# One decoder layer on one core: MLP products by one level of Strassen, projection in two column passes, activation sums kept in HBM

## What is computed

```
h   = h + concat(y_conv, y_ret) @ w_out          # 1024 x 1024
hn2 = rmsnorm(h, norm_mlp)
h   = h + square(relu(hn2 @ w_up)) @ w_down      # 1024 x 4096, 4096 x 1024
y   = rmsnorm(h, norm_final)                     # meta tokens dropped
```

## Time and profile before

| what | value |
|---|---|
| median of 3 runs | 1241.77 us (1241.03 to 1242.4) |
| span of the profiled execution, first to last instruction | 1239.3 us |
| input stages, up to the projection | 0 to 402.8 us |
| output projection | 402.8 to 493.3 us |
| MLP with the end | 493.3 to 1239.3 us |
| busy in the span: PE, DVE, ACT, POOL | 98%, 45%, 27%, 18% |
| DMA moved, mean rate | 70.35 MB, 57 GB/s |

### The profile page before, as it was taken

The page is one execution under the profiler, slowest core; times in us unless marked ns, Lnnn a source line. Parts: engine busy times, 40 slices in busy tenths (PEclk is TensorE's granted clock), DMA queues, the critical chain, the costliest instruction groups (busy, mean ns, idle before and its releaser), DMA issues.

```text
span 1239.3 us, 19873 instructions
## 1 busy us (share of the span) xinstructions
PE 1219.2 (98%) x7759; PEld 1195.8 (96%) x7759; DVE 556.0 (45%) x943; ACT 333.5 (27%) x667; POOL 224.3 (18%) x144
## 2 busy tenths in 40 slices
PE   8999999999999999999999999999999999999997
PEld 7889998999999999999999999999999999999997
DVE  4345455464455655643343343343333343343345
ACT  5412313224125333320321321311311311311324
POOL 0144243252231223911011010010010010010000
PEclk9999999999999999999999999999999999999999
DMA  5331211311311112121111111111111111111103
GB/s 190 125 86 51 71 51 35 86 51 36 85 35 37 52 34 85 34 69 51 52 50 36 51 51 47 38 51 51 34 51 51 42 43 51 51 49 36 34 18 120
DMA packets 101225, 70.35 MB, mean 57 GB/s; under 512 B 2477, under 2 KB 97417, under 8 KB 101187
## 3 DMA queue, kind: packets, MB, share of 16 engines
q1 hardware_dynamic: 96415, 67.42, 17.8%
q10 hardware_dynamic: 4772, 2.40, 0.7%
HBM read 63.18 MB, written 6.64 MB: 56 GB/s over the span
## 4 chain that ended last, share of the span: by engine, by line
PE 95%; DVE 3%; ACT 1%; issue 1%; DMA 0%; SPq 0%; POOL 0%; DVEq 0%; POOLq 0%; ACTq 0%
PE bank L1004 29%; PE bank L1006 28%; PE bank L1005 28%; PE bank L1037 1%; PE bank L1038 1%; PE bank L1040 1%; DVE state L870 1%; PE bank L1094 1%; PE bank L1099 1%; PE bank L1096 1%; PE bank L1108 1%; PE bank L1132 1%; PE bank L1201 1%; DVE rstd_b L941 1%; PE bank L1020 1%
## 5 line engine op out<-in xcount | busy, mean ns | idle before, releaser
L1004 PE MATMUL bank<-x_hi,w_hi 128*128 128x344 f32 (+2 forms) x1344 | 435.4, 324 | 2.1 <-DVE h_f L944 1.8
L1006 PE MATMUL bank<-x_hi,w_lo 128*128 128x344 f32 (+2 forms) x1344 | 430.2, 320 | 0.0
L1005 PE MATMUL bank<-x_lo,w_hi 128*128 128x344 f32 (+2 forms) x1344 | 429.5, 320 | 0.0
L1004 PEld LDWEIGHTS bank<-x_hi,w_hi 128*128 128x128 f32 x1344 | 252.2, 188 | 4.4 <-DVE w_lo L706 1.9
L1005 PEld LDWEIGHTS bank<-x_lo,w_hi 128*128 128x128 f32 x1344 | 252.5, 188 | 0.3
L1006 PEld LDWEIGHTS bank<-x_hi,w_lo 128*128 128x128 f32 x1344 | 252.5, 188 | 0.0
L1005 PE MATMUL bank<-mid_lo,w_hi 128*128 128x344 f32 (+3 forms) x720 | 230.7, 320 | 0.0
L1006 PE MATMUL bank<-mid_hi,w_lo 128*128 128x344 f32 (+3 forms) x720 | 230.3, 320 | 0.0
L1004 PE MATMUL bank<-mid_hi,w_hi 128*128 128x344 f32 (+3 forms) x720 | 229.8, 319 | 0.0
L390 POOL TENSOR_TENSOR w_raw<-w_raw,prm 128x1024 f32<-128x1024 f32 x56 | 109.3, 1957 | 590.1 <-DMA w_raw<-w_up_dram 540.7
L481 ACT ACTIVATE w_hi<-w_raw 128x1024 fp32r<-128x1024 f32 x94 | 98.9, 1053 | 378.7 <-PE bank L1006 374.3
(11 more groups left out here) (147 smaller groups left out, 1079.1 us busy)
## 6 DMA issues: line engine op xcount, KB each, us to landing
w_raw<-w_up_dram SPq DMA_DIRECT2D x32, 512.0 KB, 3.9
w_raw<-w_down_dram SPq DMA_DIRECT2D x32, 512.0 KB, 3.4
w_raw<-w_in_dram SPq DMA_DIRECT2D x28, 512.0 KB, 3.6
w_raw<-w_out_dram SPq DMA_DIRECT2D x8, 512.0 KB, 3.5
x_raw<-x_prompt_dram SPq DMA_DIRECT2D x7, 512.0 KB, 3.5
y_prompt_dram<-y_out SPq DMA_DIRECT2D x7, 512.0 KB, 2.6
state<-state_ret_dram SPq DMA_DIRECT2D x4, 512.0 KB, 5.0
v_bc<-v_smp_dram SPq DMA_DIRECT2D x4, 512.0 KB, 6.5
```

The costliest lines, as they stand in the source:

```text
L1004: m_.matmul(out, sh, mh, start=i == 0, stop=False)
L1005: m_.matmul(out, sh, ml, start=False, stop=False)
L1006: ins = m_.matmul(out, sl, mh, start=False, stop=i == len(pairs) - 1)
```

## The change

**Projection.** The 1032 columns are now two halves of 516 (HALF), and each half two parts of 258 (TQ). The projection goes over all 8 output tiles for part t = 0 of both halves, then again for part t = 1. So it loads and splits w_out twice (16 tiles, 32 groups of 24 matmuls with 258 columns). h is kept in `hid` and saved to HBM (h_dram). While the second pass runs, GpSimd, ScalarE and VectorE normalise the t = 0 part and make the seven combined operands that Strassen's method (Winograd's form) needs of it, hi and lo of each. Those of t = 1 are made in the first up passes.

**Up.** w_up and hn2 are taken as 2 x 2 blocks: hidden features by halves, input features by halves, tokens by halves. One unit is two hidden tiles (u and u + 16). GpSimd makes four sums of the weight blocks (`up_sum`), ScalarE and VectorE hi and lo of seven operands in single slots (`up_split`, `up_low`). TensorE does seven steps of 12 matmuls for each part t, accumulating in three PSUM bank pairs (BANK), and ScalarE and VectorE combine the results into the four blocks of the hidden activations while the steps go on. There are 18 passes: units 0 and 1 in two narrow passes each (one part t), units 2 to 15 in one wide pass each (both parts). After a pass ScalarE applies Relu and Square, GpSimd makes the four sums of blocks that the down products need (`mid_sum`), and SP stores the seven operands to HBM (m_dram).

**Down.** 8 blocks (of 4 hidden tiles) x 4 pairs of output tiles, 7 steps of 6 matmuls for each part. The last block is done for t = 0 first and then for t = 1. Weights are combined in the same way (`down_sum`, `down_split`, `down_low`), and the block's seven operands are loaded back from HBM through two slots (`load_mid`) and split (`mid_split`, `mid_low`). VectorE adds every step's result into the accumulators. For block 0 it adds h, loaded back from HBM, instead.

**Norm gain and factor** are applied to the activations before the up products; the gain on the weights is gone. **End:** ten groups of tokens; three are finished between the last down passes, seven after the last.

The core of the diff, in this order: constants, SP with its loads and stores, GpSimd, ScalarE (the up passes, then the down passes), VectorE (mid_low, the up passes, the down passes), TensorE (the up passes, the down passes):

```diff
+A_OP = ((0, 0), 1, (0, 1), 2, 0, (1, 1), 3)
+BANK = (0, 1, 0, 1, 2, 1, 2)
+STARTS = (True, True, False, False, True, False, False)
+UNITS = DFF // P // 2
+UP = [(0, (0,)), (1, (0,)), (1, (1,)), (0, (1,))] + [(u, (0, 1)) for u in range(2, UNITS)]
+NU = len(UP)
+UP_S = [0, 1, 1, 2] + list(range(3, NU - 1))
+BLOCKS = 8
+DN = [(b, n, (0, 1)) for b in range(BLOCKS - 1) for n in range(4)] + [(BLOCKS - 1, n, (t,)) for t in range(2) for n in range(4)]
+ND = len(DN)
...
+            def load_up(u):
+                for i in range(2):
+                    c0 = P * (u + UNITS * i)
+                    sp.dma_start(up_raw[u % 2][:, i, :, :], w_up_t[:, :, c0:c0 + P]).then_inc(up_in[u % 2], 16)
...
+            def store_rest(q):
+                u, ts = UP[q]
+                c0, c1 = TQ * ts[0], TQ * (ts[-1] + 1)
+                sp.wait_ge(mid_sums, 4 * q + 4)
+                sp.dma_start(m_dram[u, :, 1:7, c0:c1], hid[:, 1:7, META + c0:META + c1]).then_inc(rest_saved, 16)
...
+            def load_mid(m):
+                b, j = m // 7, m % 7
+                sp.wait_ge(first_saved, 16 * (2 * b + 4))
+                sp.wait_ge(rest_saved, 16 * (2 * b + 4))
+                if m >= 2:
+                    sp.wait_ge(mid_ready, 2 * m - 2)
+                sp.dma_start(m_raw[m % 2][:, :, :], m_dram[2 * b:2 * b + 2, :, j, :].rearrange("u p c -> p u c")).then_inc(mid_in[m % 2], 16)
...
+            for q in range(NU):
+                if q:
+                    store_rest(q - 1)
+                if q == 3:
+                    sp.wait_ge(up_ready, 7 * (last_pass(0) + 1))
+                    load_up(2)
+                if q >= 4:
+                    u = q - 2
+                    if u + 1 < UNITS:
+                        sp.wait_ge(up_ready, 7 * (last_pass(u - 1) + 1))
+                        load_up(u + 1)
+                if q < NU - 1:
+                    store_first(q)
+            sp.wait_ge(up_ready, 7 * NU)
+            load_down(0)
+            load_mid(0)
+            load_mid(1)
+            load_down(1)
+            for i in range(4):
+                load_h(0, i)
+            for m in range(2, 7):
+                load_mid(m)
+            store_first(NU - 1)
+            store_rest(NU - 1)
+            for wi in range(NW):
+                b, n = wi // 4, wi % 4
+                if wi + 2 < NW:
+                    sp.wait_ge(dn_ready, 7 * wi + 7)
+                    load_down(wi + 2)
+                if b < BLOCKS - 1:
+                    for j in range(2 * n, min(2 * n + 2, 7)):
+                        load_mid(7 * (b + 1) + j)
...
+            def mid_sum(q):
+                u, ts = UP[q]
+                c0, c1 = META + TQ * ts[0], META + TQ * (ts[-1] + 1)
+                b12 = hid[:, 3, HALF + c0:HALF + c1]
+                b11, t2, b21, t3, t1, t4, b22 = (hid[:, j, c0:c1] for j in range(7))
+                pool.wait_ge(mid_set, 4 * q + 4)
+                g.tensor_tensor(t1, b12, b11, ALU.subtract).then_inc(mid_sums, 1)
+                pool.wait_ge(mid_sums, 4 * q + 1)
+                g.tensor_tensor(t2, b22, t1, ALU.subtract).then_inc(mid_sums, 1)
+                g.tensor_tensor(t3, b22, b12, ALU.subtract).then_inc(mid_sums, 1)
+                pool.wait_ge(mid_sums, 4 * q + 2)
+                g.tensor_tensor(t4, b21, t2, ALU.subtract).then_inc(mid_sums, 1)
...
+            up_sum(1)
+            block_sums(1)
+            for q in range(1, NU):
+                mid_sum(q - 1)
+                if q + 1 < NU and UP_S[q + 1] != UP_S[q]:
+                    up_sum(q + 1)
+            down_sum(0)
...
+            for q, (u, ts) in enumerate(UP):
...
+                for i in range(7):
+                    if i == 0:
+                        act.wait_ge(up_done, 7 * q + 1)
+                        if q in (0, 2):
+                            act.wait_ge(normed, 8 * (ts[0] + 1))
+                            act.wait_ge(h_saved[ts[0]], 32)
+                        if q:
+                            act.wait_ge(up_read, 5 * (q - 1) + 4)
+                        s.activation(split(hid[:, 0, HALF + c0:HALF + c1]), pair[0][:, tsl, 0:TQ], ACT.Copy).then_inc(up_x_read, 1)
+                    if i == 2:
+                        act.wait_ge(up_done, 7 * q + 3)
+                        if q:
+                            act.wait_ge(mid_sums, 4 * q)
+                            act.wait_ge(first_saved, 16 * q)
+                        s.activation(split(hid[:, 0, c0:c1]), pair[0][:, tsl, 0:TQ], ACT.Relu).then_inc(up_x_read, 1)
+                        act.wait_ge(up_x_read, 2 * q + 2)
+                        s.activation(hid[:, 0, c0:c1], hid[:, 0, c0:c1], ACT.Square).then_inc(mid_set, 1)
+                    if q + 1 < NU:
+                        up_split(q + 1, i)
+                        if q == 0 and i == 2:
+                            std_rows(1)
...
+            for q, (b, n, ts) in enumerate(DN):
+                for i in range(7):
+                    if q + 1 < NW:
+                        down_split(q + 1, i)
+                    if b < BLOCKS - 1 and i in (1, 4) and 2 * n + i // 4 < 7:
+                        mid_split(7 * (b + 1) + 2 * n + i // 4)
...
+            def mid_low(m, half):
+                b, j = m // 7, m % 7
+                dve.wait_ge(mid_high, m + 1)
+                d.tensor_tensor(m_lo[b % 2][j][:, half, :], m_raw[m % 2][:, half, :], m_hi[b % 2][j][:, half, :], ALU.subtract).then_inc(mid_ready, 1)
...
+                for i in range(7):
+                    if i == 1:
+                        dve.wait_ge(up_done, 7 * q + 2)
+                        dve.wait_ge(up_x_read, 2 * q + 1)
+                        d.tensor_tensor(u2, yb, s1, ALU.add).then_inc(up_read, 1)
+                    if i == 3:
+                        dve.wait_ge(up_done, 7 * q + 4)
...
+                    if q + 1 < NU:
+                        up_low(q + 1, i)
...
+                for i in range(7):
+                    src = pair[BANK[i]][:, tsl, 0:TQ]
+                    dve.wait_ge(dn_done, 7 * q + i + 1)
...
+                    if b < BLOCKS - 1 and i in (2, 3, 5, 6) and 2 * n + i // 5 < 7:
+                        mid_low(7 * (b + 1) + 2 * n + i // 5, (i - 2) % 3)
...
+            for q, (u, ts) in enumerate(UP):
+                for i in range(7):
+                    pe.wait_ge(up_ready, 7 * q + i + 1)
+                    if i == 0:
+                        if q:
+                            pe.wait_ge(up_x_read, 2 * q)
+                        else:
+                            pe.wait_ge(h_done, GROUPS - 1)
+                    elif i == 2:
+                        pe.wait_ge(up_x_read, 2 * q + 1)
+                    elif i in (1, 4) and q:
+                        pe.wait_ge(up_read, 5 * q - (1 if i == 1 else 0))
+                    elif i == 3:
+                        pe.wait_ge(up_read, 5 * q + 1)
+                    elif i >= 5:
+                        pe.wait_ge(up_read, 5 * q + i - 3)
+                    for t in ts:
+                        if q < 4:
+                            pe.wait_ge(op_ready, 7 * t + i + 1)
+                            if t == 1 and q == 2:
+                                pe.wait_ge(h_done, GROUPS)
+                        ins = product(pair[BANK[i]][:, t, 0:TQ], [up_hi[i][:, k, :] for k in range(4)], [up_lo[i][:, k, :] for k in range(4)],
+                                      [b_hi[t][i][:, k, :] for k in range(4)], [b_lo[t][i][:, k, :] for k in range(4)], i)
+                    ins.then_inc(up_done, 1)
+                    if q == 0 and i == 1:
+                        row_sums(1)
...
+            for q, (b, n, ts) in enumerate(DN):
+                wi = q if q < NW else q - 4
+                for i in range(7):
+                    pe.wait_ge(dn_ready, 7 * wi + i + 1)
+                    pe.wait_ge(mid_ready, 14 * b + 2 * i + 2)
+                    if i == 0:
+                        if q:
+                            pe.wait_ge(dn_read, 7 * q - 4)
+                        else:
+                            pe.wait_ge(up_x_read, 2 * NU)
+                    elif i in (1, 4):
+                        if q:
+                            pe.wait_ge(dn_read, 7 * q - (1 if i == 1 else 0))
+                        else:
+                            pe.wait_ge(up_read, 5 * NU - (1 if i == 1 else 0))
+                    elif i < 4:
+                        pe.wait_ge(dn_read, 7 * q + i - 1)
+                    else:
+                        pe.wait_ge(dn_read, 7 * q + i - 1)
+                    wn = n if b == BLOCKS - 1 else 0
+                    for t in ts:
```

More of the change, by code:

```diff
@@ L896, in head @@
                 if last:
[L897 to L900 removed]
+                    y_low(rest, 0, 0, 3)
+                    y_low(rest, 1, 0, 4)
+                    for l in range(2):
+                        y_low(most, l, 1, 5 + 2 * l)
+                        y_low(rest, l, 1, 6 + 2 * l)
                 assert own[0] == OWN
@@ L994, in _ @@
+            for i in range(3, len(FINAL)):
```

(3 more changed lines are left out.)

774 lines of the change are left out of this document (492 added, 282 removed).

## The result

The changed kernel takes 1626.1 us (median, 1622.3 to 1630.9) against 1241.55 of the kernel before in the same session: a ratio of 1.310, interval 1.307 to 1.312. Slower was forecast, with 1443 us and a range to 1510, so the size is wrong by 183 us. The profiled execution has a span of 1626.6 us, 185.9 above the 1440.7 of the prediction's sum; what follows accounts for that difference. It moves 142.92 MB by DMA where the old kernel moved 70.35.

What follows compares the result with a forecast made beforehand. TensorE's matrix products were taken to bound the kernel: 1164.0 us without waits, plus waits in up and down passes and 28.9 for the clock, gave 1440.7, forecast as 1443 us, range 1375 to 1510.

Steps and rivals of the forecast that it cites:

- The products: MLP: 5376 products of 258 columns at 119.7 ns, 643.5 us; up passes 20.1 and down passes 10.06 without waits.
- rival 4: Whole kernel: the change saves no products, or the shorter ones cost as much; 1643 us, chance 0.02.
- The mechanism of the up stage: Wide up passes: weight load queued behind a store waiting for mid_sum; TensorE waits 10.9 us before step 3.
- the clock's term: Throttled clock: coming back costs about 1.7 us after each of 17 waits of 5 us or more; 28.9 us.
- Passes 0 to 2 ... 14 (5 to 20): First up passes: making the second column tile's operands, with waiting for GpSimd's block sums, costs 14 us (5 to 20).
- 2.1 us in each of 27 passes: Down stage: TensorE waits 2.1 us before step 5 for the next block's mids, 56.7 us in all.
- taken as the shorter load since its rows are long: Down stage: the loads of mids land 3.5 us after their issue.
- rival 2: Down stage: each 2.1 us wait also loses the clock, or slowed GpSimd binds; 1489 us, chance 0.15.
- GpSimd 11 steps of 0.73 inside a pass of 12.1: nothing: Down passes: GpSimd's 8.0 us of work fits inside the pass and adds no time.
- each engine below 60 us: Projection: added conversions lie under 92 us of products, each engine below 60 us, so they add nothing.
- The store's issue and landing, 3.0: Tail: issue and landing of the store take 3.0 us of the 22.6 us after the last product.
- Rival 3: Whole kernel: waits on transfers don't show and products are all there is; 1205 us, faster; chance 0.05.

Runs made afterwards that it cites:

- experiment 9: All wait-removing edits together (early loads, raw slot, split order, spread sums and low parts, later store, tail rows) against the changed kernel: 1269.2 us, ratio 1.0221 to the old kernel.
- experiment 2: Down stage's loads of the middle's raw halves issued one pass earlier, against the changed kernel: 1500.5 us.
- Experiment 6: Projection only: first hidden-state store two tiles later, VectorE's four low parts spread after tiles 1 to 4, against the changed kernel: 1614.6 us.
- experiment 7: Last six output tiles cut into other row counts (96, 80, 84 for 88, 86, 86), against the changed kernel: 1617.9 us.
- experiment 4: Up stage's raw weight load put ahead of store_rest in the same pass instead of behind it, against the changed kernel: 1448.2 us.
- experiment 8: Raw slots exchanged from unit 2 and pass 17's middle splits reordered, on the kernel with both stages' loads a pass earlier: 1311.9 us.
- experiment 5: Filler products added before step 3's wait in up passes 5 to 16 of the changed kernel: 1620.6 us with 42, 1870.4 with 150, 1587.6 with 50.

## Why the prediction was right in kind and wrong in size

- **The products: right.** 5376 products of 258 columns, 0.120 us apart; wide up passes of 20.7 and down passes of 10.1 once the loads are early, for 20.1 and 10.06 foreseen. So rival 4, whose 1643 us lies nearest to the measured 1626, is refuted all the same: the number is near by chance.
- **The mechanism of the up stage: right, and its size nearly so.** Gaps of 11.3 to 11.9 for 10.9. But the clock's term was too small: step 3 took 5.08 us for 2.76, a loss of 2.3 where 1.7 was charged, and a wide pass took 34.1 for 32.7, 17.1 us in twelve. The whole stage is 43.0 above its share. The other large part is "Passes 0 to 2 ... 14 (5 to 20)", where the passes took 66.0 for 44.2 in all, 21.8 too much: by the trace VectorE and ScalarE stand in order behind GpSimd's four block sums (2.4, 3.9, 2.9 and 3.3 us, 12.5 for the 9.8 foreseen), and GpSimd's sums of the first middle behind them again. About 9 us are steps at half clock, for which nothing was charged there. The term gave VectorE's load and no sum for the waiting on GpSimd. No run isolates this; experiment 9 spread some of these sums, and the three passes fell from 66.0 only to 63.2. Passes 3, 4 and 17 give the last 4 us.
- **The down stage is the step that failed most, by 90.6 us.** "2.1 us in each of 27 passes" was 3.3 (3.2 without the products' own pace). Of the 1.1 to 1.2 us too little, 0.3 is the issue of the mids (3.5 us into the pass for 3.2) and 0.9 their landing, 4.4 us after it instead of the 3.5 "taken as the shorter load since its rows are long"; the rest of the chain took what was foreseen. And the clock, charged for none of these waits, fell in 21 of the 27 passes. That was rival 2. Wait and clock together make these passes 71.9 us longer than the sum had them. I gave rival 2 0.15 and priced it as all or nothing with the wait still at 2.1; experiment 2 gives 4.7 us for wait and clock together. Down pass 0 gives 3.2 more, and the last block 15.5 (11.6 of it in passes 28 to 31): "GpSimd 11 steps of 0.73 inside a pass of 12.1: nothing" holds for the 28 passes ahead of it and not for passes 28 to 31, which are half as long (5.3 us) but need a whole weight each.
- **The projection: "nothing" was 35.0 us.** The argument was "each engine below 60 us" under 92 us of products. VectorE had 74.5 us of work there and GpSimd 69.0, so the premise was wrong; but neither is more than 92, and the load alone explains no gap. The queues are in order: four low parts that nobody needs for some 45 us (until group 16) stood ahead of one that was needed at once, and a store ahead of a load. Experiment 6 shows both.
- **The tail: 39.9 for 22.6.** "The store's issue and landing, 3.0" came from stores of 128 rows. Those of 86 rows take over 10 us (issued at 1597.1 and 1600.2, landed when VectorE went on at 1607.3 and 1613.8). With other rows experiment 7 measures 23.3, near the forecast.
- **What stayed right of the clock:** it falls in each wide pass and nowhere where nothing waits. What was wrong is the list: 17 waits were charged, while the profile shows it in the projection (4 groups), in passes 0 to 2, in 21 of 27 down passes and in the last block (passes 30 and 31) too. So the clock was 0.79 over the up stage where "near 0.9" was foreseen.
- The sum of these: 35.0 + 43.0 + 90.6 + 17.3 = 185.9 us, the difference from the span.

The direction, given 0.94, came out. Rival 3 is answered by the runs, not by the result: with the waits of the wide up passes and of down passes 1 to 27 gone the kernel takes 1323 and at best 1269, never the 1205 worked out for it, because the projection, up passes 0 to 3 and 17, down pass 0, the last block and the tail cost more than its sum had for them.

## What to carry to other kernels

A change that saves an eighth of the products adds sums, splits and round trips, and each engine's idle share says nothing about them: read each in-order queue (SP's above all) for what is needed late but stands ahead of what is needed now. Two statements exchanged in SP's queue gave back 178 us here. Price a wait near 3 us with the clock's loss behind it, since at that size it may be paid or not from pass to pass; and cut tail tiles into row counts that move fast (experiment 7).

## What the runs showed of the hardware that was not expected

- A store of 86 rows moved at 40 to 53 GB/s with 0.11 to 0.13 of the DMA engines busy; two of them took 10.2 and 13.6 us until VectorE had the buffer back. With tiles of 80, 84 and 96 rows VectorE never waits more than 1.5 us for it (experiment 7).
- SP's issues are not always 0.5 us: two loads behind a 1.5 MB store took 2.67 us of the queue (1.19 in experiment 4, issued 4.9 us behind such a store), and four weight loads 4.20 in experiment 8 (1.91 in down pass 9).
- The granted clock fell late. In experiment 5 it was 1.00 through 3.2 us of stillness (771.4 to 774.6) and 0.61 over the products behind it. Gaps of 1.3 us in the last down passes didn't cost it. Of gaps of 2.1 to 3.6 us some did and some didn't: 2.06 before group 24 of the projection did, 2.17 before group 6 in experiment 6 did not, and of the 27 down passes 21 lost it (gaps of 2.8 to 5.1) and 6 kept it (2.8 to 3.6).
- The same low part (128x512) takes VectorE 0.69 us at 751.3 and 1.14 and 1.03 at 768.6 and 771.6, where GpSimd's sums run beside it. The runs didn't isolate this.
